# Routing stage of a two-layer MoE trunk: TensorE's shared-expert slices, position counts, table products and down products in another order

## The reference, cut to what matters

```
scores = sigmoid(x @ router_w)                       # 512 x 64
idx    = top_k(scores + router_bias, 8)              # 8 experts for each token
gate   = scores[idx] / sum(scores[idx]) * 2.5
# every expert's tokens are laid into blocks of 128 rows
for each block (tok, e):
    y = (silu(x[tok] @ w_gate[e]) * (x[tok] @ w_up[e])) @ w_down[e] * gate
    routed[tok] += y
shared = (silu(x @ sw_gate) * (x @ sw_up)) @ sw_down
x = layernorm(ALPHA * x + routed + shared)
```

## Time and profile before

| | |
|---|---|
| median of 3 runs | 2452.58 us (2445.71 to 2452.81) |
| the profiled execution | 2453.17 us |
| its span, first to last instruction | 2451.5 us |
| outside the span | 1.67 us |
| PE busy | 2286.8 us, 93% |
| DVE busy | 1604.3 us, 65% |
| ACT busy | 1085.8 us, 44% |
| POOL busy | 696.8 us, 28% |
| routing stage, layer 0 / layer 1 | 77.6 us / 76.9 us |

### The profile page before, as it was taken

The page is one execution under the profiler, slowest core; times in us unless marked ns, Lnnn a source line. Parts: engine busy times, 40 slices in busy tenths (PEclk is TensorE's granted clock), DMA queues, the critical chain, the costliest instruction groups (busy, mean ns, idle before and its releaser), DMA issues.

```text
span 2451.5 us, 32999 instructions
## 1 busy us (share of the span) xinstructions
PE 2286.8 (93%) x9437; PEld 1623.4 (66%) x9437; DVE 1604.3 (65%) x1753; ACT 1085.8 (44%) x1251; POOL 696.8 (28%) x704
## 2 busy tenths in 40 slices
PE   7949889999999999959999999997999999999994
PEld 4413557777667667649988888555677777776673
DVE  4874557767667666652377888546677776776675
ACT  3552125555555555422233334212555555555551
POOL 4970213344433433300000000002233343343331
PEclk9969889999999999979999999988999999999997
DMA  6210359999999999733322221333999999999994
GB/s 219 69 34 0 129 202 338 372 376 373 362 353 359 358 354 365 252 121 109 89 75 75 81 78 52 104 120 129 337 359 367 372 366 361 365 372 353 360 367 139
DMA packets 195965, 592.57 MB, mean 242 GB/s; under 512 B 25357, under 2 KB 95093, under 8 KB 160580
## 3 DMA queue, kind: packets, MB, share of 16 engines
q1 hardware_dynamic: 163796, 517.79, 56.5%
q0 software_dynamic: 32112, 74.05, 12.5%
HBM read 579.16 MB, written 51.38 MB: 257 GB/s over the span
## 4 chain that ended last, share of the span: by engine, by line
PE 79%; DMA 8%; DVE 5%; ACT 1%; issue 1%; SPq 0%; POOLq 0%; POOL 0%; DVEq 0%; ACTq 0%
PE PS L1443 27%; PE PS L1464 18%; PE PS L1601 11%; DMA W<-in_exp_w_down 6%; PE PS L1534 6%; PE PS L1329 4%; PE PS L1430 4%; PE PS L1368 2%; PE PS L1452 1%; PE PS L1642 1%; PE PS L1617 1%; PE PS L1414 1%; DMA acc<-BIG,IDXS 1%; PE PS L1387 1%; PE PS L1348 1%
## 5 line engine op out<-in xcount | busy, mean ns | idle before, releaser
L1048 DVE TENSOR_TENSOR WL<-W,WH 128x2048 fp32r<-128x2048 f32 x276 | 621.1, 2292 | 197.5 <-ACT WH L700 184.6
L700 ACT ACTIVATE WH<-W 128x2048 fp32r<-128x2048 f32 x276 | 512.3, 1907 | 42.5 <-DVE IDX L1026 42.5
L1464 PE MATMUL PS<-W,BIG 128*128 128x512 f32 x1104 | 499.3, 595 | 10.5 <-issue 4.5
L1443 PE MATMUL PS<-WH,XH 128*128 128x512 f32 x1104 | 446.8, 405 | 8.8 <-DVE XL L1041 8.8
L1443 PE MATMUL PS<-WH,XL 128*128 128x512 f32 x1104 | 435.1, 394 | 0.0
L1443 PE MATMUL PS<-WL,XH 128*128 128x512 f32 x1104 | 432.8, 392 | 0.0
L594 POOL DMA_INDIRECT acc<-BIG,IDXS x138 | 265.8, 1926 | 464.7 <-issue 391.6
L1464 PEld LDWEIGHTS PS<-W,BIG 128*128 128x128 f32 x1104 | 199.2, 190 | 213.4 <-issue 204.8
L710 ACT ACTIVATE BIG<-PS 128x512 f32<-128x512 f32 x138 | 83.0, 601 | 363.6 <-PE PS L1464 361.1
L1443 PEld LDWEIGHTS PS<-WH,XH 128*128 128x128 f32 x1104 | 209.5, 190 | 48.4 <-DVE XL L1041 9.6
L1443 PEld LDWEIGHTS PS<-WH,XL 128*128 128x128 f32 x1104 | 209.2, 189 | 46.0
(11 more groups left out here) (240 smaller groups left out, 3056.4 us busy)
## 6 DMA issues: line engine op xcount, KB each, us to landing
W<-in_exp_w_gate SPq DMA_DIRECT2D x138, 1024.0 KB
W<-in_exp_w_up SPq DMA_DIRECT2D x138, 1024.0 KB
W<-in_exp_w_down SPq DMA_DIRECT2D x138, 1024.0 KB
RAW<-in_w_kv SPq DMA_DIRECT2D x48, 512.0 KB, 3.8
RAW<-in_attn_w_q SPq DMA_DIRECT2D x24, 512.0 KB, 3.8
W<-in_conv_w_in SPq DMA_DIRECT2D x8, 1024.0 KB, 11.4
acc<-BIG SPq DMA_DIRECT2D x9, 512.0 KB, 3.7
W<-in_conv_w_out SPq DMA_DIRECT2D x4, 1024.0 KB, 6.6
```

Source lines behind the costliest of these rows:

```text
L700: A(WH[:, s, c, :], W[:, 3 - 3 * s + c, :], ACT.Copy).then_inc(s_wh[l], 1)
L1048: v.tensor_tensor(WL[s][:, c, :], W[:, 3 - 3 * s + c, :], WH[:, s, c, :].bitcast(F32), ALU.subtract).then_inc(s_wl[l], 1)
L1443: last = mm(PS[:, 3 + s, :].rearrange("p (a b) -> p a b", a=2), a, w, start=(k == 0 and i == 0), stop=(k == KT - 1 and i == 2))
L1464: last = mm(PS[:, 5 + h, :], HTm[:, s, k * P:(k + 1) * P], wd[:, k, h * 512:(h + 1) * 512], start=(k == 0), stop=(k == 1))
```

## The change

On PE, `sh_gate_up` takes the range of its eight steps, so that it can be cut. The first four steps of slice 0 come ahead of the position counts, two between the counts and the overflow bases, the last two and slice 1 behind these. The table products become a function for one slice: slices 0 and 1 stand ahead of `sh_down(1)`, slices 2 and 3 behind it. `sh_down(3)` moves behind `rows_T(0, 0, 0)`, and with it the wait for all of `s_sye`. On ACT, the copy of the first block's rows (`rows_high(0, 0)`) moves ahead of `shared_down(3)`, and a sigmoid of one column whose result nobody reads is added behind the last square root of `norm_round(0)` and `norm_round(2)`. DVE, POOL and SP keep their streams. The operations of PE are the same in number and kind.

```diff
@@ scalar, norm_round(r)
                     A(std1[:, :], mv[:, 1:2], ACT.Sqrt, bias=eps[:, :]).then_inc(s_nstd, 1)
+                    if r % 2 == 0 and n == NT - 1:
+                        A(scratch[:, 9:10], eps[:, :], ACT.Sigmoid)
@@ scalar, moe(l)
                 shared_gate_up(3)
                 shared_down(2)
+                rows_high(0, 0)
                 shared_down(3)
                 act.wait_ge(s_ax[1], 2 * l + 2)
                 act.wait_ge(s_xr[l], 16 * NT)
-                rows_high(0, 0)
@@ tensor, moe(l)
-                sh_gate_up(0)
-
+                def tables(n):
+                    pe.wait_ge(s_pj[l], n + 1)
+                    for j in range(8):
+                        last = mm(PS[:, 0, 256:256 + 2 * NB], PJ[:, n % 2, j, :], RR[:, n % 2, j, :],
+                                  start=(n == 0 and j == 0), stop=(n == NT - 1 and j == 7))
+                    last.then_inc(s_tb[l], 1)
+
+                sh_gate_up(0, range(4))
                 pe.wait_ge(s_mk, l + 1)
...
                 last.then_inc(s_pos, 1)
-                sh_gate_up(1)
+                sh_gate_up(0, range(4, 6))
                 pe.wait_ge(s_cb, l + 1)
...
+                sh_gate_up(0, range(6, KT))
+                sh_gate_up(1)
                 sh_down(0)
                 sh_gate_up(2)
+                tables(0)
+                tables(1)
                 sh_down(1)
-
-                for n in range(NT):
-                    pe.wait_ge(s_pj[l], n + 1)
-                    for j in range(8):
-                        last = mm(PS[:, 0, 256:256 + 2 * NB], PJ[:, n % 2, j, :], RR[:, n % 2, j, :],
-                                  start=(n == 0 and j == 0), stop=(n == NT - 1 and j == 7))
-                    last.then_inc(s_tb[l], 1)
+                tables(2)
+                tables(3)
                 sh_gate_up(3)
                 sh_down(2)
-                sh_down(3)
 
                 pe.wait_ge(s_tab, 2 * l + 2)
-                pe.wait_ge(s_sye[l], 2 * NT)
...
                 rows_T(0, 0, 0)
+                sh_down(3)
+                pe.wait_ge(s_sye[l], 2 * NT)
                 gate_up(0, 0)
```

More of the change, by code:

```diff
@@ L1360, in moe, with sh_gate_up @@
             def moe(l):
-                def sh_gate_up(n):
-                    if n == 0:
+                def sh_gate_up(n, ks=range(KT)):
+                    if n == 0 and ks[0] == 0:
                         landed(pe, ("sg", l))
@@ L1366, in sh_gate_up @@
                         pe.wait_ge(s_ssl[l], 2 * (n - 1))
-                    for k in range(KT):
+                    for k in ks:
                         last = mm(PS[:, 4 + n % 2, :].rearrange("p (a b) -> p a b", a=2), XT[:, k, n * P:(n + 1) * P],
                                   pair(("sg", l), k), start=(k == 0), stop=(k == KT - 1))
-                    last.then_inc(s_sgu[l], 1)
+                    if ks[-1] == KT - 1:
+                        last.then_inc(s_sgu[l], 1)
                 def sh_down(n):
```

## The result

The changed kernel takes 2423.87 us (median of 4 runs, 2417.91 to 2429.17) against 2452.47 for the kernel before: a ratio of 0.9887 with a 95% interval of [0.9866, 0.9908], 28.6 us less. The forecast was 2435.5 with a range from 2429 to 2446. The profiled execution of the changed kernel is its quickest run, 2417.91 us with a span of 2416.2, 35.3 us less than the profiled one before.

What follows compares the result with a forecast made beforehand. It took PE to bound the kernel, with some 13 us idle per routing stage plus half clock. Reordering was to gain 8.5 us a layer, 17 in all, from 2452.58 to 2435.5 us; range 2429 to 2446.

Steps and rivals of the forecast that it cites:

- steps 1 and 2: Layer 0's routing on PE: counts end 3.5 us earlier, then bases earlier, so obs comes at 279.1, 8.9 us earlier.
- step 3: DVE's chain from obs to first one-hots: 20.25 us kept whole or 18.3 without the POOL collision; second slice at 301.0 to 303.0.
- step 5: End of the routing stage: gate_up at 336.75 to 337.75 instead of 345.75, a gain of 8.0 to 9.0 us a layer.
- more than the sum: Rival: PE reaches the blocks without its clock falling, up to 3 us more a layer, 23 in all, 2430; chance 0.04.
- The sum: Main case for both routing stages: 8.5 us a layer, 17 us in all (13 to 21), 2432 to 2440; chance 0.70.
- The register load: PE's block-count load ahead of rows_T, behind eight queued matmuls: costs 0 to 0.96 us.
- One-hots late: Rival: POOL also collides with DVE's second slice, tables(1) waits 3.9 us; gain 9 us in all, 2443; chance 0.07.
- Clock falling ahead of sh_down(3): Rival: half clock around the new rows_T doubles sh_down(3)'s 3.70, gain about 10 us in all, 2443; chance 0.07.
- rows_T waiting for rows: Rival: a late gather holds rows_T and sh_down(3), PE waits 5.7 us; gain 5.6 in all, 2447; chance 0.08.
- Loop DMA-bound: Rival: all 138 expert-loop blocks wait for weights; at 0.25 us a block 2470; chance 0.04.

Runs made afterwards that it cites:

- e4: The full change without the added sigmoid in the norm: 2426.89 us against 2452.07 for the kernel before, ratio 0.9888.
- e1: The kernel before with only slice 0's shared gate/up cut and the counts and bases earlier: 2438.47 us against 2452.07, ratio 0.9938.
- e8: The full change plus two unused products on PE in the gap ahead of gate_up(0, 0): 2423.22 us against 2452.90 before, ratio 0.9871.
- e5: The full change measured once more, for its spread: 2425.21 us against 2452.90 for the kernel before, ratio 0.9891.
- e2: The kernel before with only the table products split around sh_down(1): 2447.78 us against 2452.07, ratio 0.9981.

## Why the prediction was right and where it was wrong

**What held.** The chain of cause did: PE's order, not DVE's speed, made obs late. obs was forecast for 279.1 and came at 277.92, in a stage that began 0.76 earlier. Tables without a wait, rows_T right behind sh_down(2), sh_down(3) at 3.70, and the sigmoid worth nothing (e4) all came as written. e1, which is steps 1 and 2 alone, took 13.6 us off the median. That the tables had no wait was in part luck. Tables(1) didn't wait although the collision of L1010 stayed, because another one, on the fourth L986, went; the forecast did not have it. With the chain of 20.25 us kept whole, as step 3 had it at the late end, slice 1 would have been ready at 301.8, about a microsecond after PE wanted it (my estimate, from 299.21 and the 2.62 by which the chain was shorter).

**The step that failed** is in the last sentence of step 5: "I leave the half-clock start of the blocks (clock 0.80) as it is." It is not a constant of the kernel. Of the layers profiled with the change's tail some take 18.9 us for the first blocks and some 23.2, 4.3 us apart: 2.7 to 2.9 of it behind the first gap and 1.6 behind the second. The forecast had this as its rival "more than the sum" at 0.04, and at 3 us a layer, where its own row, 23.25 us at 0.80, gives up to 4.65. It deserved a large share of the chance: the rows that it rested on showed the fall behind two idle stretches around light work (1.63 and 2.55), and the change left one of 3.2.

That alone doesn't explain the miss: the profiled run of e4 had both falls in both layers and took 2428.06 us, still 1 us below the range. The sum was short as well.

**Terms that were mis-sized**, all the same way. From the first shared product to gate_up I had 68.6 to 69.6 us; it is 66.5. The counts started after 5.2 and not 5.9 us (0.7; in other runs between 0 and 0.8). Tables 2.6 a slice and not 2.8 (0.8 in all). sh_down 4.4 to 4.7 and not 4.8 (0.5). The register load ahead of rows_T cost 0 and not 0 to 0.96: 324.48 is where sh_down(2)'s stream ends. Durations of groups include the drain of the last instruction, and I took them for distances between starts. Together with the spread of the start this is 1.8 to 2.6 us a layer beyond the 8.5.

**The account**, profiled executions: 35.3 us = 21.4 in the two routing stages (17 forecast) + 8.6 in the first blocks (0 forecast) + 5.3 elsewhere. For the medians it is 28.6: about 21, plus between 0 and 8.6 as the clock falls, and what is left is within the spread of the later blocks. From the hidden transpose of the tenth block to that of the last they took 587.2 to 595.2 us in layer 0 and 602.5 to 609.1 in layer 1 over fourteen profiles, with 590.3 and 604.1 before; PE's own waits for down weights make a part of that (6.7 us in e8's layer 0, 1.1 in the change's, 2.7 before). They don't give back what the first blocks gain: behind first blocks of 18.9 us they took 588.1 and 605.6 us on average, behind first blocks of 22 or more 589.7 and 605.5. Whether the change takes anything from these blocks stays open, as does what lets the clock fall at one gap and not at its twin.

**The rivals.** One-hots late: the collision of 2.58 us was there, but slice 1 was ready 1.5 us ahead of PE, with the luck told above. The instruction that was held, L1010 (now L1012), has one tensor input and not two, as the prediction's sentence on the one-hots has it; the three before it have two, and ran at their usual 0.95 to 1.23 us. Clock falling ahead of sh_down(3): 3.70 us in every profile, so out. rows_T waiting for rows: out, they landed within 6.9 us (317.60 to 324.48). Loop DMA-bound: out, 1.9 us of waits for down weights in layer 0 against 4.4.

**What adds up.** From counts to gate_up the early counts are worth 2.9 us a layer alone, and the way to the counts is 4.2 and 3.3 shorter; the split is worth 0.8 alone and 3.2 with the early counts; the tail 0.5 to 0.8 either way. The split only pays once DVE's chain is early enough.

## What to carry to other kernels

When one engine feeds a long chain on another, cut its independent work into pieces and put just enough of them in front of each hand-over to cover its latency; regrouping products further down pays only after that. When a stage loses idle time on TensorE, look up each stretch behind a gap in the windows for its granted clock, and give the clock there a term and a chance of its own: here it was worth up to 8.6 us beside the 21 of the reordering. And take distances between starts, not durations, when laying out a stream of matmuls.

## What the runs showed of the hardware

- The same PE stream took 61.33, 61.33, 61.33 us from counts to gate_up in layer 0 of three executions (the change, e4, e5), and then 18.9 or 23.2 us behind a gap of 3.25 us, with a granted clock of 1.00 or 0.80 (full and half are 2.4 and 1.2 GHz). One execution did both, in its two layers.
- More work on PE made the kernel quicker: fillers in the kernel before, 12.1 us; in the change, about 7.
- With the first of two gaps filled the clock still fell behind the second, of 1.82 us (e8: 18.9 expected, 20.5 measured).
- Before, 0.96 us passed between the end of ACT's copy and rows_T, which the forecast puts down to the register load; with eight products queued ahead of the same load there is no pause (324.48).
- A DVE instruction that met POOL's add L624 (2.35 to 2.97 us) took 2.58 us for 0.62 (L1010) or 2.86 for 0.68 (L986). PE's order decides which one meets it: both before, L1010 alone in the change, L986 alone in e2.
